# Rotary partners by buffer transfers instead of products with a constant matrix, in a two-block transformer kernel

## The chip, the cores and the metric

The kernel runs on one core of one Trainium2 chip. The metric is the device time of one execution in microseconds (us), as the median of three runs. The core has five engines that run side by side and wait for one another by semaphores: TensorE (PE, matrix products, with its weight loads as PEld), VectorE (DVE), ScalarE (ACT), GpSimd (POOL) and SyncE (SP). Transfers (DMAs) are issued by SP, ACT and POOL and carried out by 16 DMA engines that all queues share.

## The reference, cut to what matters

A sequence of 256 tokens with 1024 features goes through one block without rotary embedding and then through two layers (`l` = 0, 1), each of feed-forward, token mixer, feed-forward. The token mixer has three attention kinds of 8 heads: MOBA (here causal softmax attention), stick-breaking (SB) and latent attention (MLA). Rotary embedding is applied in two of them:

```python
def apply_rope(x, cos, sin):
    x1, x2 = jnp.split(x, 2, axis=-1)
    return jnp.concatenate([x1 * cos - x2 * sin, x1 * sin + x2 * cos], axis=-1)

def partial_rope(x, cos, sin):            # MOBA queries and keys: the first 16 of a head's 64 features
    return jnp.concatenate([apply_rope(x[..., :PARTIAL_ROT], cos, sin), x[..., PARTIAL_ROT:]], axis=-1)
# MLA: apply_rope on the 32 rotary features of each head's query, and on 32 features of a key that all heads share
```

Each rotated feature needs its partner: the feature 8 places away in MOBA (16 in MLA). The output is x * cos + partner * (plus or minus sin).

## The kernel before

Activations of a layer are kept with features on the 128 partitions and the 256 tokens along each partition. Moving a value to its partner feature therefore means moving it between partitions, which VectorE and ScalarE do not do in an elementwise operation. The kernel before does it with TensorE: it multiplies by a 128x128 matrix of 0, 1 and -1 (`rot_p` for MOBA, `rot_m` for MLA, both part of the constant block `dcon`), into the PSUM tile `nps`.

Weights come in chunks of 1 MB. SP loads chunk c into `raw` (three buffers). ACT rounds it to `hi` (`split`, L816), DVE subtracts to get `lo` (`split`, L1179), PE does three products per tile pair (hi x hi, hi x lo, lo x hi: L429 to L431), 48 matmuls of 256 columns for a chunk. The order on each engine is written out by hand; nothing is reordered by a scheduler.

In the token mixer, chunks and heads are interleaved in steps s (`mixing`). Ahead of step 0 stand the chunks `moba.q0`, `moba.k0`, `moba.v0`, `moba.q1` (each q or k chunk gives 256 features, that is 4 heads, as a 128x512 tile of `ra`; `v` is values). In step s PE does: the scores of head s (in pairs at even s), the value products of finished heads, the turning of the normalized weights of head s-1 (`turned`, L694, a transposition through `pt`), and then one weight chunk of the list: `moba.k1` in step 0, `moba.v1` in step 1, then the SB chunks, the latent chunks `lat.0` and `lat.1` (steps 8, 9), gates, `uq` in step 13 (MLA queries), `ukv` in step 14 (MLA keys and values). ACT and DVE treat the chunk of the step before: ACT copies it out of PSUM (`take`, L940 to L945), splits the chunk after next, does `exps` (L976) of head s and copies `pt` for head s-1 (L989). DVE does `largest` (L1336: adds the mask and takes the row minimum), its half of `split`, then whatever the dictionary `extra` names for this step, then `normed` (L1348, L1355: divides by the row sums), and some products for the modulation vectors (L1195, 1024 elements each).

The rotary steps stand in this frame as follows.

- PE: `rotary_moba` (L730) for q0 after `fm_first`, for k0 after the chunk v0, for q1 in step 0, for k1 in step 1. `rotary_mla` for the key in step 12 (L743) and for the query in step 14 (L748). All six share `nps`, so each waits for the rotation before it.
- DVE: `rotate_moba` (L1416 to L1419, three operations of 128x512: partner by sine, value by cosine, sum) for q0 and k0 before step 0, for q1 and k1 in steps 0 and 1 between `split` and `normed`. `rotate_mla_k` (L1423) in step 12, `rotate_mla_q` (L1430) in step 14, ahead of `take_v` (L1410), which empties the PSUM banks of `ukv` that PE needs for the next chunk but one.
- Who waits: the scores of head 0 wait for the rotation of k0, those of head 4 for k1. The turning of head 0 on PE waits for `normed` of head 0, which stands behind the rotation of q1 on DVE; the turning of head 1 waits for `normed` of head 1, behind the rotation of k1.

POOL issues the bias loads of the first block (L408) and, for each of eight vectors, a store to DRAM and a broadcast load back (L395, L402).

Of the kernel before, what the change touches and what calls it, by code (L numbers as in the profile page):

```python
# [10 lines left out]
ALU = mybir.AluOpType  # L11

P = 128
SEQ = 256
# [3 lines left out]
HD = 64  # L18
# [118 lines left out]
DCOL, NDCOL = columns(("neg_tri", P), ("neg_ones", P), ("rot_p", P), ("rot_m", P), ("cos_p", SEQ),  # L137
# [21 lines left out]
def program(nc, d, known):  # L159

    with ExitStack() as ctx:
# [85 lines left out]
        s_cond_b_in = signal("cond_b_in")  # L247
        s_out_stored = signal("out_stored")
# [4 lines left out]
        s_summed, s_rotated, s_across = signal("summed"), signal("rotated"), signal("across")  # L253
# [13 lines left out]
        s_glu = signal("glu")  # L267
# [10 lines left out]
        def flat2(ap):  # L278
            return ap.rearrange("p a t -> p (a t)")
# [23 lines left out]

        def values_of(l, kind):
            return m_v if kind == "mla" else qkv_of(l, kind)[2]

# [82 lines left out]
        def _(eng):  # L389
            nc.gpsimd.memset(eps[:], EPS).then_inc(*s_eps_made.up("eps"))  # L390
            def turned_row(tag, cols):
# [8 lines left out]
                if tag[2:] == "post1":  # L400
                    eng.wait_ge(*s_scored.at((tag[0], 3 * HEADS - 1)))
# [23 lines left out]
        def _(eng):  # L425
# [297 lines left out]
            def rotary_moba(l, n):  # L723

                c = AT[f"{l}.moba.{n}"]
                eng.wait_ge(*s_taken_a.at((c, 0)))
                if n != "q0":
                    eng.wait_ge(*s_rot.at((l, {"k0": "q0", "q1": "k0", "k1": "q1"}[n])))
                at = 4 * (n[0] == "k") + 2 * int(n[1])
                mm(nps[:], dcon[:, DCOL["rot_p"]], flat2(ra[:, at:at + 2, :]), start=True,  # L730
                   stop=True).then_inc(*s_rotated.up((l, n)))

# [6 lines left out]

            def rotary_mla(l, what):  # L740
                if what == "k":
                    eng.wait_ge(*s_r.at(l + ".lat"))
                    mm(nps[:, 0:SEQ], dcon[:, DCOL["rot_m"]], lat[:, 3, :], start=True,  # L743
                       stop=True).then_inc(*s_rotated.up((l, "mla k")))
                else:
                    eng.wait_ge(*s_taken_a.at((AT[f"{l}.uq"], 0)))
                    eng.wait_ge(*s_rot.at((l, "mla k")))
                    mm(nps[:], dcon[:, DCOL["rot_m"]], flat2(m_qr), start=True,  # L748
                       stop=True).then_inc(*s_rotated.up((l, "mla q")))
# [1080 lines left out]
```

## Time and profile before

| what | value |
|---|---|
| median of 3 runs | 1740.6 us (1739.4 to 1741.92) |
| profiled execution, its own time | 1739.8 us |
| its span | 1738.0 us |
| mean granted TensorE clock | 0.997 of full |
| PE busy | 1673.2 us, 96% |
| PEld busy | 1552.6 us, 89% |
| DVE busy | 1258.4 us, 72% |
| ACT busy | 875.1 us, 50% |
| POOL busy | 21.8 us, 1% |
| chain that ended last, by engine | PE 80%, DVE 6%, ACT 5%, DMA 3%, others 5% |

The span is the time from the first to the last instruction of the profiled execution; its own time is 1.8 us longer. The chain that ended last follows, from the last instruction back, what released each step. In the rows further down, each timeline row has the start in us from the span's start, the duration in us, engine, line, operation, and `output<-inputs`; `x2` is two instructions merged into the row, and the bracket at the end is idle time of that engine just before, with what ended it. Layer 0's mixer starts near 640 us, layer 1's near 1290 us, and the rows of the two are alike.

### The profile page before, as it was taken

The numbers are of one execution on the slowest core, as the hardware profiler recorded it, in microseconds if no ns is written. First come the engines' busy times: TensorE is split into PE (matmuls) and PEld (weight loads), VectorE is DVE, ScalarE is ACT, GpSimd is POOL, SyncE is SP. The second block draws the span as 40 slices with busy tenths as digits, with TensorE's granted clock in tenths as the row PEclk, the third lists the DMA queues.
The fourth block names the chain that finished last, engine by engine and source line by source line (L and its number), as shares of the span: only waits on it lengthen the run. The fifth ranks groups of instructions, "written<-read, shape, count | busy, mean of one in ns | idle before, by whom it ended". The sixth has DMA issues, their size and how long they took to land.

```text
span 1738.0 us, 29616 instructions
## 1 busy us (share of the span) xinstructions
PE 1673.2 (96%) x12356; PEld 1552.6 (89%) x12356; DVE 1258.4 (72%) x1813; ACT 875.1 (50%) x1241; POOL 21.8 (1%) x39
## 2 busy tenths in 40 slices
PE   2999999998999999999999999999999999999998
PEld 2999889987999889989989998999889989989996
DVE  6777879987787666666768875787666666768653
ACT  4555466654444365665473344534365665464432
POOL 0000000000000000000000000000000000000000
PEclk9999999999999999999999999999999999999999
DMA  9868646777677944755548786677744746537552
GB/s 384 309 254 247 241 168 236 208 294 280 217 290 280 289 171 170 209 191 200 214 146 290 283 240 241 229 282 288 291 162 169 220 180 214 205 147 272 186 179 108
DMA packets 70933, 398.92 MB, mean 230 GB/s; under 512 B 8208, under 2 KB 8464, under 8 KB 36112
## 3 DMA queue, kind: packets, MB, share of 16 engines
q1 hardware_dynamic: 67392, 386.06, 63.1%
q0 software_dynamic: 2976, 9.47, 1.6%
q8 instruction: 98, 1.61, 0.4%
q10 hardware_dynamic: 432, 1.50, 0.2%
q14 instruction: 35, 0.29, 0.0%
HBM read 395.92 MB, written 1.08 MB: 228 GB/s over the span
## 4 chain that ended last, share of the span: by engine, by line
PE 80%; DVE 6%; ACT 5%; DMA 3%; DVEq 2%; issue 2%; ACTq 1%; SPq 1%
PE lin L429 17%; PE lin L430 17%; PE lin L431 17%; PE att L564 17%; DVE lo L1179 3%; ACT hi L816 2%; PE att L667 2%; PE lin L467 2%; DMA raw<-in_w 2%; PE lin L469 2%; DMA ada_w<-in_ada 2%; PE lin L477 2%; DVEq L1508 1%; PE pt L694 1%; SPq L355 1%
## 5 line engine op out<-in xcount | busy, mean ns | idle before, releaser
L1179 DVE TENSOR_TENSOR lo<-raw,hi 128x2048 fp32r<-128x2048 f32 x262 | 600.1, 2291 | 288.6 <-ACT hi L816 288.4
L429 PE MATMUL lin<-h_hi,hi 128*128 128x256 f32 x2480 | 699.2, 282 | 2.4 <-DVE work L1503 1.6
L430 PE MATMUL lin<-h_lo,hi 128*128 128x256 f32 x2480 | 691.9, 279 | 0.0
L431 PE MATMUL lin<-h_hi,lo 128*128 128x256 f32 x2480 | 691.9, 279 | 0.0
L816 ACT ACTIVATE hi<-raw 128x2048 fp32r<-128x2048 f32 x262 | 500.5, 1911 | 209.7 <-PE att L564 133.6
L429 PEld LDWEIGHTS lin<-h_hi,hi 128*128 128x128 f32 x2480 | 466.3, 188 | 5.3 <-issue 5.1
L430 PEld LDWEIGHTS lin<-h_lo,hi 128*128 128x128 f32 x2480 | 466.3, 188 | 1.1 <-issue 1.0
L431 PEld LDWEIGHTS lin<-h_hi,lo 128*128 128x128 f32 x2480 | 466.1, 188 | 0.0
L1195 DVE CUSTOM_DVE_ANT_0 ada_w<-ada_w,cs 128x1024 f32<-128x1024 f32 x179 | 218.0, 1219 | 18.7 <-DMA ada_w<-in_ada 18.6
L1032 ACT ACTIVATE work<-lin 128x256 f32<-128x256 f32 x88 | 33.9, 385 | 280.1 <-PE lin L431 271.9
L564 PE MATMUL att<-hi,act_hi 128*128 128x512 f32 x440 | 135.6, 389 | 0.2 <-DVE lo L1179 0.2
L564 PE MATMUL att<-lo,act_hi 128*128 128x512 f32 x440 | 135.5, 389 | 0.0
L564 PE MATMUL att<-hi,act_lo 128*128 128x512 f32 x440 | 135.5, 389 | 0.0
L564 PEld LDWEIGHTS att<-lo,act_hi 128*128 128x128 f32 x440 | 82.6, 188 | 17.2
L564 PEld LDWEIGHTS att<-hi,act_lo 128*128 128x128 f32 x440 | 82.6, 188 | 17.2
L564 PEld LDWEIGHTS att<-hi,act_hi 128*128 128x128 f32 x440 | 82.1, 188 | 17.3 <-DVE lo L1179 0.6
L467 PE MATMUL lin<-h_hi,hi 128*128 128x256 f32 x240 | 59.4, 289 | 21.1 <-ACT h_hi L897 21.1
L467 PEld LDWEIGHTS lin<-h_hi,hi 128*128 128x128 f32 x240 | 46.9, 195 | 23.0 <-issue 23.0
L429 PE MATMUL lin<-br_hi,hi 128*128 128x256 f32 x224 | 64.1, 286 | 1.9 <-ACT ra L952 1.6
L430 PE MATMUL lin<-br_lo,hi 128*128 128x256 f32 x224 | 62.5, 279 | 0.0
L431 PE MATMUL lin<-br_hi,lo 128*128 128x256 f32 x224 | 62.5, 279 | 0.0
L469 PE MATMUL lin<-h_hi,lo 128*128 128x256 f32 x240 | 58.6, 285 | 0.0
(266 smaller groups left out, 2015.5 us busy)
## 6 DMA issues: line engine op xcount, KB each, us to landing
raw<-in_w SPq DMA_DIRECT2D x269, 1024.0 KB, 4.8
ada_w<-in_ada SPq DMA_DIRECT2D x179, 512.0 KB, 5.2
ada_s<-in_ada SPq DMA_DIRECT2D x13, 512.0 KB, 16.5
bias<-in_bias POOLq DMA_DIRECT2D x16, 256.0 KB, 4.7
ffn_row<-rows POOLq DMA_DIRECT2D x5, 512.0 KB, 9.7
x<-in_x ACTq DMA_DIRECT2D x1, 1024.0 KB, 6.8
dcon<-in_dcon SPq DMA_DIRECT2D x1, 1024.0 KB, 6.9
ra<-rows POOLq DMA_DIRECT2D x2, 512.0 KB, 5.0
```

Of the source, the lines that this page charges most:

```text
L429: mm(out, w_hi, a_hi, start=start, stop=False, skip_group_check=skip)
L430: mm(out, w_hi, a_lo, start=False, stop=False, skip_group_check=skip)
L431: return mm(out, w_lo, a_hi, start=False, stop=stop, skip_group_check=skip)
L467: mm(o, hi[c % SPLIT][:, b], h_hi[:, t, :], start=t == 0 and j == 0, stop=False, skip_group_check=True)
L469: mm(o, lo[c % SPLIT][:, b], h_hi[:, t, :], start=False, stop=False, skip_group_check=True)
L477: ins = mm(outs[i][:, j * SEQ:(j + 1) * SEQ], hi[c % SPLIT][:, b], h_lo[:, t, :], start=False, stop=t == 3, skip_group_check=True)
L564: ins = mm(att[:, 2 * a + n, :], act[:, t, tokens], w[s][:, kk * D + n * 512:kk * D + (n + 1) * 512], start=t == 0 and i == 0, stop=t == 2 ...
L667: ins = mm(out, q, k, start=start, stop=stop, skip_group_check=skip)
L816: act(hi[c % SPLIT][:], raw[:, c % RAW, :], ACT.Copy).then_inc(*s_hi.up(c))
L1032: act(work[2 + k % 2][:, 0:SEQ], lin[:, BANK[(c, 0)], 0:SEQ], ACT.Silu).then_inc(*s_gated.up((stage, k)))
L1179: tt(lo[c % SPLIT][:], raw[:, c % RAW, :], hi[c % SPLIT][:].bitcast(F32), ALU.subtract).then_inc(*s_lo.up(c))
L1195: ve.tensor_tensor_reduce(out=w, in0=w, in1=cs[:], scale=1.0, scalar=0.0, op0=ALU.mult, op1=ALU.add, accum_out=ada_out[:, h:h + 1]).then_i ...
```

## The change

The partner features are no longer a product. They are copied between partitions by small DMAs inside SBUF, and the sine table now carries the sign (negative for the first half of the rotated features).

- MOBA: for each of q0, k0, q1, k1, ACT issues four DMAs (`fetch_moba`), each of 8 partitions by 512 values (16 KB), from `ra` into `turn` (queries) or `lat_sq` (keys). They stand in ACT's order after the split that follows the chunk's `take`; for q1 and k1 they stand at the end of steps 0 and 1 (`late`), behind `exps`, and in step 1 also behind the copy of `pt`.
- MLA: POOL issues eight DMAs of 16 partitions for the key (256 values each) once `lat.1` is taken, and eight for the query (512 values each) once the first part of `uq` is taken, into free rows of `ra`. They stand between the store and the broadcast load of the row `post1`.
- DVE: `rotate` waits for the last of the DMAs instead of the product, and multiplies the partner tile in place, out of SBUF instead of PSUM. Since the MOBA transfers write only 16 of every 64 partitions, `clear_partners` sets `turn` and `lat_sq` to zero once per layer, after the last `swiglu` of the first feed-forward. `take_v` gets a `drain` in front.
- PE: `rotary_moba` and `rotary_mla` are gone, and with them the matrices in `dcon` (256 of its 2048 columns).

ACT, around steps 0 and 1 of the mixer. Before (`L940` and `L943` are the takes of q1 and k1, `L816` the split, `L976` the exps, `L989` the copy of `pt`):

```order
L940 ACTIVATE ra<-lin 128x512
L816 ACTIVATE hi<-raw 128x2048
L976 ACTIVATE work,den<-work,mn 128x128
L976 ACTIVATE work,den<-work,mn 128x256
L943 ACTIVATE ra<-lin 128x512
L816 ACTIVATE hi<-raw 128x2048
L976 ACTIVATE work,den<-work,mn 128x128
L976 ACTIVATE work,den<-work,mn 128x256
L989 ACTIVATE work<-pt 128x384
```

The same place after the change:

```order
L935 ACTIVATE ra<-lin 128x512
L811 ACTIVATE hi<-raw 128x2048
L988 ACTIVATE work,den<-work,mn 128x128
L988 ACTIVATE work,den<-work,mn 128x256
L947 DMA turn<-ra 8x512 x4
L938 ACTIVATE ra<-lin 128x512
L811 ACTIVATE hi<-raw 128x2048
L988 ACTIVATE work,den<-work,mn 128x128
L988 ACTIVATE work,den<-work,mn 128x256
L1001 ACTIVATE work<-pt 128x384
L947 DMA lat_sq<-ra 8x512 x4
```

Four transfers now follow the exps of head 0, and four follow the copy of `pt` in step 1.

PE, end of the chunk q1 and start of step 0. Before (`L667` are the scores of heads 0 and 1, `L730` the product with `rot_p` for q1, `L429` and `L430` the chunk k1):

```order
L431 MATMUL lin<-h_hi,lo 128x256
L667 MATMUL att<-ra 128x128 x2
L667 MATMUL att<-ra 128x256 x2
L730 MATMUL nps<-ra,dcon 128x512
L429 MATMUL lin<-h_hi,hi 128x256
L430 MATMUL lin<-h_lo,hi 128x256
```

After the change:

```order
L451 MATMUL lin<-h_hi,lo 128x256
L687 MATMUL att<-ra 128x128 x2
L687 MATMUL att<-ra 128x256 x2
L449 MATMUL lin<-h_hi,hi 128x256
L450 MATMUL lin<-h_lo,hi 128x256
L451 MATMUL lin<-h_hi,lo 128x256
```

Only the product is gone; the order of the rest stays.

The diff, cut to its core:

```diff
         @block.gpsimd
+            def fetch_mla(l, what):
+                eng.wait_ge(*s_taken_a.at((AT[f"{l}.lat.1" if what == "mla_k" else f"{l}.uq"], 0)))
+                src = lat[:, 3:4, :] if what == "mla_k" else m_qr
+                for to, fro, n, last in partner_rows(MLA_ROPE, MLA_ROPE):
+                    eng.dma_start(partner_of[what][to:to + n], src[fro:fro + n]).then_inc(
+                        *s_partner[what].up(*([(l, what)] if last else []), n=16))
...
                 if tag[2:] == "post1":
+                    fetch_mla(tag[0], "mla_k")
+                    fetch_mla(tag[0], "mla_q")
                     eng.wait_ge(*s_scored.at((tag[0], 3 * HEADS - 1)))
...
         @block.tensor
                 fm_first(l + ".pre1", f"{l}.moba.q0", f"{l}.moba.k0")
-                rotary_moba(l, "q0")
                 tm(f"{l}.moba.v0")
-                rotary_moba(l, "k0")
                 fm(f"{l}.moba.q1")
-                mixing(l, MIX_HEADS, MIX_SLOTS, {
-                    0: lambda: rotary_moba(l, "q1"), 1: lambda: rotary_moba(l, "k1"), 11: lambda: latent_sums(l),
-                    12: lambda: rotary_mla(l, "k"), 14: lambda: rotary_mla(l, "q")})
+                mixing(l, MIX_HEADS, MIX_SLOTS, {11: lambda: latent_sums(l)})
...
         @block.scalar
+            def fetch_partners(l, what, src):
+                dst, arrived = partner_of[what.split(".")[0]], s_partner[what.split(".")[0]]
+                for to, fro, n, last in partner_rows(16, HD):
+                    eng.dma_start(dst[to:to + n], src[fro:fro + n]).then_inc(
+                        *arrived.up(*([(l, what)] if last else []), n=16))
+
+            def fetch_moba(l, n):
+                c = AT[f"{l}.moba.{n}"]
+                at = 4 * (n[0] == "k") + 2 * int(n[1])
+                if n[1] == "0":
+                    eng.wait_ge(*s_cleared.at(l))
+                else:
+                    eng.wait_ge(*s_rot.at((l, n[0] + "0")))
+                eng.wait_ge(*s_taken_a.at((c, 0)))
+                fetch_partners(l, f"{n[0]}.{n[1]}", ra[:, at:at + 2, :])
...
                 for n in ("q0", "k0", "v0"):
                     take(f"{l}.moba.{n}")
                     split(AT[f"{l}.moba.{n}"] + SPLIT)
+                    if n != "v0":
+                        fetch_moba(l, n)
...
+                    0: [lambda: fetch_moba(l, "q1")], 1: [lambda: fetch_moba(l, "k1")],
                     9: [square_q], 10: [square_kv], 11: [latent_r], 12: [latent_first],
...
         @block.vector
+            def rotate(l, what, x_, cos, sin, done):
+                partner = partner_of[what.split(".")[0]]
+                n = x_.shape[1]
+                eng.wait_ge(*s_partner[what.split(".")[0]].at((l, what)))
+                tt(partner, partner, over(dcon[:, DCOL[sin]], n), ALU.mult)
+                tt(x_, x_, over(dcon[:, DCOL[cos]], n), ALU.mult)
+                ve.drain()
+                return tt(m_kr.unsqueeze(1) if what == "mla_k" else x_, x_, partner, ALU.add).then_inc(
+                    *s_rot.up((l, done)))
...
+            def clear_partners(l):
+                ve.memset(turn[:], 0.0)
+                ve.memset(lat_sq[:, 0:2, :], 0.0).then_inc(*s_cleared.up(l))
```

## Rows read from the trace of the kernel before

**Rows 1.** Head of the page.
```profile
span 1738.0 us, 29616 instructions
```

**Rows 2.** PE timeline, layer 0: products for q0 and k0, and a matmul behind.
```profile
640.62 1.02 PE L730 MATMUL nps<-ra,dcon 128*128 128x512 f32 x2
...
641.60 0.28 PE L430 MATMUL lin<-lo,h_hi 128*128 128x256 f32 x1
...
648.09 1.10 PE L730 MATMUL nps<-ra,dcon 128*128 128x512 f32 x2 [0.77 <-ACT ra L945]
```

**Rows 3.** PE timeline, steps 0 to 2: scores, turning of head 0, k1's product, turning of head 1.
```profile
654.72 0.93 PE L667 MATMUL att<-ra 64*128 64x128 f32 x8
...
662.28 0.55 PE L694 MATMUL pt<-con,work 128*128 128x128 f32 x3
663.04 1.12 PE L730 MATMUL nps<-ra,dcon 128*128 128x512 f32 x2 [0.22 <-ACT ra L943]
...
670.63 0.55 PE L694 MATMUL pt<-con,work 128*128 128x128 f32 x3
```

**Rows 4.** DVE timeline, k0's rotation and step 0.
```profile
653.35 0.69 DVE L1419 TENSOR_TENSOR ra<-ra,turn 128x512 f32<-128x512 f32 x1
655.67 0.29 DVE L1336 CUSTOM_DVE_ANT_0 work<-att,con 128x128 f32<-128x128 f32 x1 [1.63 <-PE att L667]
...
656.24 0.08 DVE L1336 DVE_READ_ACCUMULATOR2_ANT mn<- 128x1 f32 x1
657.25 2.29 DVE L1179 TENSOR_TENSOR lo<-raw,hi 128x2048 fp32r<-128x2048 f32 x1 [0.93 <-ACT hi L816]
659.46 0.68 DVE L1416 TENSOR_TENSOR turn<-nps,dcon 128x512 f32<-128x512 f32 x1
...
661.67 0.55 DVE L1355 TENSOR_SCALAR work<-work,rden 128x128 f32<-128x128 f32 x2
```

**Rows 5.** ACT timeline, first and last row of the exps of head 0.
```profile
657.12 0.39 ACT L976 ACTIVATE work<-work,mn 128x128 f32<-128x128 f32 x1
...
657.91 0.19 ACT L976 ACTIVATION_READ_ACCUMULATOR work<-work,mn 128x1 f32 x1
```

**Rows 6.** ACT's queue at the start: its first and third DMA issue.
```profile
0.73 0.41 ACTq L1040 DMA_DIRECT2D x<-in_x  x1
...
1.66 0.45 ACTq L1042 DMA_DIRECT2D con<-in_con  x1
```

**Rows 7.** From issue to landing of the stores `out_x` (256 and 512 KB).
```profile
DMA to landing us min/median/max: 2.6/2.6/2.7
```

**Rows 8.** From issue to landing of POOL's bias loads (256 KB, weight loads beside them).
```profile
DMA to landing us min/median/max: 2.7/4.7/8.6
```

**Rows 9.** DVE timeline, end of the latent step (12).
```profile
750.67 0.95 DVE L1446 TENSOR_TENSOR br_lo<-lat,br_hi 128x768 fp32r<-128x768 f32 x1
```

**Rows 10.** PE timeline, first matmul of the chunk `uq`.
```profile
751.84 0.36 PE L429 MATMUL lin<-br_hi,hi 128*128 128x256 f32 x1
```

**Rows 11.** PE's waits from 742 to 768 us: total, times, longest.
```profile
PE lin L429 <- ACT ra L958: 0.8, 1, 0.8
```

**Rows 12.** ACT timeline, the takes of the first two parts of `uq`.
```profile
755.04 1.08 ACT L952 ACTIVATE ra<-lin 128x512 f32<-128x512 f32 x2
```

**Rows 13.** DVE timeline, first operation of the MLA query's rotation.
```profile
763.36 0.68 DVE L1430 TENSOR_TENSOR turn<-nps,dcon 128x512 f32<-128x512 f32 x1
```

**Rows 14.** POOL's bias DMAs: durations min/median/max in ns.
```profile
L408 POOL DMA_DIRECT2D bias<-in_bias x16: 539/539/678, 29.7 to 144.5; - x16
```

**Rows 15.** POOL timeline, stores of the rows `post0` and `post1`.
```profile
568.29 0.92 POOL L395 DMA_DIRECT2D rows<-post_gain  x1 [218.28 <-DVE post_gain L1231]
...
719.73 0.91 POOL L395 DMA_DIRECT2D rows<-post_gain  x1 [140.00 <-DVE post_gain L1231]
```

**Rows 16.** DVE timeline, the operation beside the second store.
```profile
719.35 1.22 DVE L1195 CUSTOM_DVE_ANT_0 ada_w<-ada_w,cs 128x1024 f32<-128x1024 f32 x1
```

**Rows 17.** DVE timeline, the place where the partner tiles will be cleared.
```profile
569.32 2.29 DVE L1179 TENSOR_TENSOR lo<-raw,hi 128x2048 fp32r<-128x2048 f32 x1 [1.32 <-ACT hi L816]
```

More of the change, by code:

```diff
@@ L247, in program @@
         s_cond_b_in = signal("cond_b_in")
+        s_partner = {n: signal(f"partner_{n}") for n in ("q", "k", "mla_k", "mla_q")}
         s_out_stored = signal("out_stored")
@@ L266, in program @@
         s_z, s_scaled, s_h_hi_v = signal("z"), signal("scaled"), signal("h_hi_v")
[L267 removed]
+        s_glu, s_cleared = signal("glu"), signal("cleared")
         s_act, s_taps, s_merged, s_rot, s_lat = (signal("act_made"), signal("taps"), signal("merged"), signal("rot"),
@@ L302, in program, with partner_rows @@
         m_v = ra[:, 11:15, :].rearrange("p a t -> p (a t)").rearrange("p (u n) -> p u n", u=2)
+        partner_of = {"q": turn[:], "k": lat_sq[:, 0:2, :], "mla_k": ra[:, 14:15, :], "mla_q": ra[:, 12:14, :]}
         def values_of(l, kind):
             return m_v if kind == "mla" else qkv_of(l, kind)[2]
+        def partner_rows(n_rot, width):
+            half = n_rot // 2
+            moves = [(base + to, base + half - to, half) for base in range(0, P, width) for to in (0, half)]
+            return [m + (i == len(moves) - 1,) for i, m in enumerate(moves)]
         def by_token(ap):
@@ L721, in values @@
                 ins.then_inc(*s_pv.up((l, s + 1)))
[L723 to L731, printed above, removed]
             def latent_sums(l):
@@ L738, in latent_sums @@
                 mm(nps[:, SEQ:2 * SEQ], ones, sq[:, 2, :], start=True, stop=True).then_inc(*s_summed.up(l + ".lat"))
[L740 to L749, printed above, removed]
             def mixing(l, heads, slots, extra):
@@ L1587, in _ @@
                 layer_post(l, 0)
+                clear_partners(l)
                 for k in range(FD - 1):
@@ L1662, in constants, with rotary @@
     c[:, DCOL["neg_ones"]] = -1.0
-    def rotary(n_rot, width, rot, cos, sin):
+    def rotary(n_rot, width, cos, sin):
         inv = (f(500000.0) ** (-np.arange(0, n_rot, 2, dtype=f) / n_rot)).astype(f)
@@ L1671, in rotary @@
             for r in range(n_rot):
-                row, partner = base + r, base + (r + half) % n_rot
-                m[partner, row] = -1.0 if r < half else 1.0
-                cc[row], ss[row] = np.cos(ang[:, r % half]), np.sin(ang[:, r % half])
-        c[:, DCOL[rot]], c[:, DCOL[cos]], c[:, DCOL[sin]] = m, cc, ss
-    rotary(16, HD, "rot_p", "cos_p", "sin_p")
-    rotary(MLA_ROPE, MLA_ROPE, "rot_m", "cos_m", "sin_m")
+                row = base + r
+                cc[row], ss[row] = np.cos(ang[:, r % half]), np.sin(ang[:, r % half]) * (-1 if r < half else 1)
+        c[:, DCOL[cos]], c[:, DCOL[sin]] = cc, ss
+    rotary(16, HD, "cos_p", "sin_p")
+    rotary(MLA_ROPE, MLA_ROPE, "cos_m", "sin_m")
     short = lambda m: np.concatenate([m.T[0:P, :], m.T[P:, P:]], 1)
```

25 lines of the change are left out of this document (6 added, 19 removed).

## The prediction

> **What bounds the kernel now.** I read the shares first: TensorE is busy for 96% of the span and carries 80% of the chain that ended last, so a microsecond taken from PE is worth a microsecond, unless what PE then waits for is not ready. Then the timelines of PE, DVE and ACT around the places that the change touches, in layer 0, and last the landing times of the transfers. The reader should see that PE has almost no idle time around steps 0 and 1, but that the engines behind it are only just in time: DVE's `normed` of head 0 ends at 662.22 us (661.67 + 0.55) and PE starts to turn that head at 662.28 [rows 3, 4]. All sums are made in layer 0 and taken twice. The profiled execution took 1739.8 us (span 1738.0 us [rows 1] and 1.8 us around it), the median of the runs is 1740.6 us; I add my difference to the median.
>
> **What goes from PE.** The product for q0 starts at 640.62 us, and the second matmul behind it at 641.60 us; with 0.12 us for the first one, it holds PE for 0.86 us, in two records of the trace [rows 2]. k0 costs the same and 0.77 us of waiting for ACT's take in front [rows 2]; q1 the same; k1 the same and 0.22 us of waiting [rows 3]. That is 4 x 0.86 + 0.99 = 4.4 us for each layer, 8.9 us in all. MLA follows below. Whether any of it reaches the end depends on who is late next, so I rebuild steps 0 and 1.
>
> **Before step 0.** PE reaches the chunk v0 0.86 us earlier, and ACT's take of v0, DVE's split and the rotation of k0 all follow it. The rotation ended at 654.04 us (653.35 + 0.69) [rows 4]; it will end at 653.2 us. PE will be through the chunk q1 at 654.7 - 0.86 - 0.86 - 0.77 = 652.2 us and wait 1 us. The scores of heads 0 and 1 start at 653.25 us instead of 654.72 us [rows 3]: 1.5 us won of 2.5 us. The transfers for q0 and k0 are asked for 4 us and more after they are issued, behind DVE's splits, so I cost them at nothing. ACT's issues lie beside its split if its queue goes on while the split runs; if not, ACT falls 1.8 us behind for each four, and 0.8 us of the gain goes.
>
> **Step 0.** From the scores to the turning of head 0, PE needed 662.28 - 654.72 = 7.56 us [rows 3], without the product 6.6 us (here it took nearer 0.97 us), so PE is ready at 659.85 us. DVE: `largest` ended at 656.32 us; 1.47 us earlier is 654.85 us. Before, the exps started at 657.12 us because ACT was still in its split (its `hi` came for DVE at 657.25 us [rows 4]); that split follows the chunk q1 and now ends at 654.7 us, so the exps start at 654.95 us. DVE's split runs from 654.95 to 657.2 us. The four transfers for q1 stand behind the exps, which take 1.0 us (657.12 to 658.10 [rows 5]). First issue: between 655.0 us, if ACT's queue runs ahead, and 655.95 us; I take 655.5. Issues follow each other by (1.66 - 0.73) / 2 = 0.465 us [rows 6], so the fourth is issued 1.4 us later, at 656.9 us.
>
> How long until it lands? No row shows a copy inside SBUF. Stores of 256 KB on quiet engines land after 2.6 us [rows 7]; at the rate of about 400 GB/s they would need 0.65 us for the data, which leaves an estimate of 1.95 us for a small one. Loads of 256 KB on a second queue beside weight loads land after 2.7 to 8.6 us, 4.7 in the middle [rows 8]. I take 2.3 us, between the estimate and the quiet row, since a 16 KB piece is nearer to these; the bounds are 1.95 and 4.7 us. The Trainium skill, page "DMA: Bandwidth & Descriptors", section "Anatomy of one DMA — SWDGE (gpsimd) path", gives a fixed part of about 2.0 us for each DMA; that is for the GpSimd path, no run here shows it for SBUF to SBUF, and the sum with it would be 0.3 us for each of the two waits, 1.2 us in all, below mine.
>
> So the partner lands at 659.2 us, and DVE, free since 657.2, waits 2 us. From the start of the rotation to the end of `normed` it needs 662.22 - 659.46 = 2.76 us [rows 4]: 661.95 us instead of 662.22. PE, ready at 659.85, waits 2.1 us, and is then ahead by only 0.3 us. Nearly all that was won up to here is given back.
>
> **Step 1.** Call the end of `normed` T. DVE does `largest` to T + 0.6 and its split to T + 2.9. ACT does the exps of head 1 and the copy of `pt` from T + 0.65 to T + 2.0, with the transfers for k1 behind them: first issue between T + 0.7 and T + 2.0, I take T + 1.3. The fourth lands at T + 1.3 + 1.4 + 2.3 = T + 5.0, `normed` of head 1 ends at T + 7.75. PE took 670.63 - 662.28 = 8.35 us from one turning to the next [rows 3], without the product and its wait 7.25 us. It waits 0.5 us and gains 0.6 us. With 0.3 us from step 0 this is 0.9 us ahead; I round to 1.0 us a layer, with bounds from the placing of the first issue and the landing: -2.3 us (both early, 1.95 us) to +4 us (4.7 us). From step 2 on PE is bound as before, so this difference stays.
>
> **MLA.** The key's product (half as long, 0.43 us) stands before a chunk that is followed by `uq`. But `uq` starts at 751.84 us, and what it needs, DVE's `br_lo`, ends at 751.62 us [rows 9, 10]: 0.1 us is won. The eight transfers were issued 20 us before. The query's product (0.86 us) stands before `ukv`, where PE waits 0.8 us for ACT to empty a bank [rows 11]; ACT's order does not get earlier, so the wait grows by what the product frees: nothing won. POOL's eight query transfers start when ACT's take ends at about 755.65 us [rows 12]. At 0.54 us each [rows 14] the last is issued at 759.45 us and lands at 761.8 us; DVE asks at 763.36 us [rows 13]. If it comes later, `take_v` behind it is late, and PE with it. The drain in `take_v` costs under 0.1 us. MLA together: 0, between -0.2 and +3 us a layer.
>
> **Clearing.** Two memsets of 128x512, at the length of the 128x512 operations of DVE at most 0.69 us each [rows 4], fall at a place where DVE waits 1.32 us for ACT [rows 17]. Without that cover they would delay one split by 1.4 us, in a stage in which each split is followed by another wait for ACT. Nothing. The shorter `dcon` load is far ahead of its use: nothing.
>
> **Sum.** -1.0 us a layer, -2.0 us in all: 1737.8 us by the profiled execution, 1738.6 us by the median. 8.9 us of PE work leave and about 7 us of it turn into waits for the partner's way through ACT's queue, DMA and DVE.
>
> **Rivals.**
> A. The partners are there when DVE asks. Then `normed` of head 0 ends at 657.2 + 2.76 = 659.95 us, 2.3 us earlier, and in step 1 DVE's own chain (T + 7.3 against 7.25) gives another 1.1 us: 3.4 us a layer, 6.8 in all, 1733.8 us. For it: DMA engines are lightly used here. Against it: four issues in a row behind the exps leave the landing less than 1 us.
> B (slower). The small pieces queue behind the 1 MB weight loads. Place: DVE's waits for q1 and k1. Landing at 4.7 us [rows 8] instead of 2.3 adds 2.4 us at each of four waits: +9.6 - 2.0 = +7.6, 1748.2 us. The change turns into a loss above 2.8 us of landing time, and a measurable one above 3.7 us. Against it: by my times the weight load of each step is issued after the pieces.
> C (slower). POOL's query transfers are late. If its issues wait while DVE runs operations with two inputs (a split of 2.3 us and one of 1.2 us fall there), the last lands near 766.3 us, 3 us late: +6 - 2 = +4, 1744.6 us. Against it: POOL's store beside exactly such an operation took 0.91 us, and one with DVE idle 0.92 us [rows 15, 16]. The Trainium skill, page "SBUF — State Buffer", section "SBUF: two separate sides", says that GpSimd and VectorE share a port pair as an exclusive lock, and that VectorE in some operations keeps GpSimd from writing descriptors; the rows speak against it for this operation, so by them it gets a small chance.
> D. ACT stalls at its issues and other small losses eat the rest: within 1 us of before, 1740.6 us.
>
> **Chances.** Forecast 0.48, A 0.18, B 0.15, C 0.10, D 0.09. A measurement of this kernel can tell 0.2%, 3.5 us, from no change. The forecast's own range is 1736 to 1741 us: mostly the same, with 0.10 faster. A counts as faster; of B 0.11 and of C 0.07 as slower; D as the same. Faster 0.28, same 0.54, slower 0.18. The range 1733.5 to 1745 us takes in A, C and the weak half of B.
>
> **What would show it.** In the profile after: DVE's first operation of the q1 rotation waits for a DMA by 1 to 3 us, in both layers, and PE waits about 2 us for `normed` before it turns head 0, and near 0.5 us before head 1. PE waits about 1 us for k0's rotation ahead of the scores. No wait stands before the MLA rotations, the key's and the query's. The PE rows of L730, L743 and L748 are gone, while the stretch from the chunk v0 to the turning of head 1 is shorter by about 1 us only. It would be wrong if DVE finds the partner there (A), if its waits are over 3.5 us (B), if the MLA query's rotation waits (C), or if another place than these moves by over 1 us.

## The result and the profile after

The changed kernel takes 1756.8 us (median of 4 runs, 1754.2 to 1762.0) beside 1741.3 us (4 runs, 1739.4 to 1743.4) of the kernel before on the same chip: the ratio is 1.0098, with a 95% interval from 1.0080 to 1.0117. It is 15.6 us slower, where 2 us faster was forecast and 1745 us was the upper end of the range.

The page after starts with the span (before: [rows 1]) and shows one thing that is new: the clock granted to TensorE has a dip to 8 in two of the 40 slices, one in each layer's mixer.

```profile
span 1760.2 us, 29638 instructions
...
PEclk9999999999999998999999999999998999999999
```

This profiled execution, 1762.0 us, was the slowest of the four, and some 6 us of its difference lie outside the mixers, so I compare stretches and not ends. POOL's stores of the modulation rows stand in both traces: one ahead of the mixer and one in step 8, past the four MOBA rotations ([rows 15]: 568.29 and 719.73 us); the row load at the end of the MLA heads closes a second stretch (a row is read as start, length, engine, line, operation, and in brackets the idle time before it with what ended it). That load before, on POOL's timeline:

```profile
820.60 0.54 POOL L402 DMA_DIRECT2D ra<-rows  x1 [99.95 <-PE att L667]
```

The POOL timeline after:

```profile
571.06 0.91 POOL L413 DMA_DIRECT2D rows<-post_gain  x1 [219.62 <-DVE post_gain L1246]
...
730.38 0.91 POOL L413 DMA_DIRECT2D rows<-post_gain  x1 [148.55 <-DVE post_gain L1246]
...
766.49 3.81 POOL L406 DMA_DIRECT2D ra<-ra  x8 [21.91 <-ACT ra L964]
831.46 0.58 POOL L422 DMA_DIRECT2D ra<-rows  x1 [61.16 <-PE att L687]
```

The same two stretches in every kernel of this study, both layers, in us (of one profiled execution each; the ratio is of all runs):

| kernel | store to store, layer 0 / 1 | store to row load, layer 0 / 1 | timed, ratio to before (95%) |
|---|---|---|---|
| before | 151.4 / 151.4 | 100.9 / 100.5 | 1 |
| changed | 159.3 / 158.3 | 101.1 / 101.9 | 1.0098 (1.0080 to 1.0117) |
| e1_load_waits | 151.8 / 149.7 | 101.2 / 101.2 | 1.0020 (1.0011 to 1.0029) |
| e2_no_moba_copies | 148.3 / 148.3 | 101.1 / 100.7 | 0.9975 (0.9964 to 0.9986) |
| e3_pe_kept_busy | 158.4 / 156.3 | 102.4 / 104.0 | 1.0100 (1.0083 to 1.0117) |
| e4_rotate_later | 148.2 / 147.6 | 101.7 / 101.1 | 0.9965 (0.9952 to 0.9978) |
| e5_fetch_early | 153.6 / 148.2 | 101.2 / 100.9 | 0.9997 (0.9984 to 1.0009) |
| e6_last_piece_only | 148.9 / 148.0 | 101.2 / 101.4 | 0.9980 (0.9971 to 0.9990) |
| e7_mla_only | 151.4 / 151.3 | 103.8 / 100.8 | 1.0022 (1.0014 to 1.0031) |
| e8_pool_and_later | 146.4 / 146.3 | 100.3 / 100.3 | 0.9936 (0.9923 to 0.9950) |
| e9_products_later | 150.9 / 150.9 | 100.8 / 100.6 | 0.9987 (0.9978 to 0.9996) |
| e10_pool_only | 149.5 / 148.7 | 101.4 / 101.3 | 0.9980 (0.9971 to 0.9988) |
| e11_later_from_scalar | 147.2 / 146.0 | 100.3 / 100.3 | 0.9939 (0.9925 to 0.9952) |

So the loss is 7.9 and 6.9 us in the stretch with the MOBA rotations, 0.2 and 1.4 us in MLA's: 16.4 us together, the timed 15.6. Inside that stretch in layer 0, the DVE timeline answers to [rows 4]:

```profile
655.89 0.69 DVE L1436 TENSOR_TENSOR ra<-ra,lat_sq 128x512 f32<-128x512 f32 x1
657.60 0.29 DVE L1351 CUSTOM_DVE_ANT_0 work<-att,con 128x128 f32<-128x128 f32 x1 [1.01 <-PE att L687]
...
658.16 2.29 DVE L1194 TENSOR_TENSOR lo<-raw,hi 128x2048 fp32r<-128x2048 f32 x1
665.65 0.69 DVE L1433 TENSOR_TENSOR turn<-turn,dcon 128x512 f32<-128x512 f32 x1 [5.21 <-DMA turn<-ra]
...
667.86 0.55 DVE L1370 TENSOR_SCALAR work<-work,rden 128x128 f32<-128x128 f32 x2
...
676.91 0.69 DVE L1433 TENSOR_TENSOR lat_sq<-lat_sq,dcon 128x512 f32<-128x512 f32 x1 [5.74 <-DMA lat_sq<-ra]
```

DVE waits 5.2 and 5.7 us for the last piece of q1 and of k1 (5.2 and 5.4 in layer 1). PE, where [rows 3] have no wait before L694, pays for it (L714 is that line now):

```profile
656.64 0.93 PE L687 MATMUL att<-ra 64*128 64x128 f32 x8 [1.78 <-DVE ra L1436]
668.47 0.90 PE L714 MATMUL pt<-con,work 128*128 128x128 f32 x3 [5.11 <-DVE work L1370]
676.91 0.93 PE L687 MATMUL att<-ra 64*128 64x128 f32 x8
679.73 0.55 PE L714 MATMUL pt<-con,work 128*128 128x128 f32 x3 [1.90 <-DVE work L1370]
```

When were the pieces issued? ACT's timeline (ACTq: its issues), with SP's issue of the next weight chunk beneath:

```profile
642.44 3.23 ACTq L947 DMA_DIRECT2D turn<-ra  x4
645.71 0.60 ACT L938 ACTIVATE ra<-lin 128x512 f32<-128x512 f32 x1 [1.56 <-issue]
...
658.34 0.63 ACTq L947 DMA_DIRECT2D turn<-ra  x1
...
659.00 0.63 ACTq L947 DMA_DIRECT2D turn<-ra  x1
...
659.66 1.29 ACTq L947 DMA_DIRECT2D turn<-ra  x2
```

```profile
660.47 11.05 SPq L360 DMA_DIRECT2D raw<-in_w  x2
```

The fourth piece is issued at about 660.32 us (659.66 plus the spacing of 0.66), 0.15 us ahead of the 1 MB weight load. In step 1 even the issue of the load comes first, by 0.25 us: the fourth piece goes at 670.13 + 2 x 0.66 = 671.45 us.

```profile
670.13 1.97 ACTq L947 DMA_DIRECT2D lat_sq<-ra  x3
671.20 0.33 SPq L360 DMA_DIRECT2D raw<-in_w  x1
```

Back in step 0, the DMA view of 656 to 668 us, in slices of 0.3 us, shows what became of that lead:

```profile
DMA  0289999990002020209048999999600000000000
GB/s 0 109 355 437 410 437 437 437 437 0 0 0 55 0 48 7 48 7 218 0 191 328 382 410 437 437 437 410 280 21 0 0 0 0 0 0 0 0 0 0
```

The first three pieces' bytes move at 659.6, 660.2 and 660.8 us, about 1.3 us after each issue. By that the fourth is due near 661.6 us, but the load's first bytes come at 661.4 us (218 GB/s), 0.9 us after its issue, and then the full stream to 664.6 us. By queue (q1 is SP's, q10 ACT's; packets, MB, share of the engines' time), first from 661.3 to 664.5 us, where q10 has no packet, then from 664.5 to 665.6 us:

```profile
q1 hardware_dynamic: 123, 1.01, 87.7%
```

```profile
q1 hardware_dynamic: 21, 0.04, 9.6%
q10 hardware_dynamic: 16, 0.02, 4.2%
```

All 16 packets of a 16 KB piece move behind the stream, from 664.57 us on. DVE is released at 665.65 us. A lead at the issue was no lead at the engines. Where the piece stands in the meantime the trace does not show; it shows only when packets move.

### The profile page after: what moved, and what is told of

Same layout as the page of the kernel before. It is cut to its first block, busy times and chain, and to the rows that moved or that the text cites. A ratio compares the mean times of both kernels' runs of the same rounds, so it can differ in the third digit from the quotient of the medians.

```text
span 1760.2 us, 29638 instructions
## 1 busy us (share of the span) xinstructions
PE 1675.0 (95%) x12332; PEld 1558.3 (89%) x12332; DVE 1260.1 (72%) x1817; ACT 875.7 (50%) x1241; POOL 37.2 (2%) x71
## 4 chain that ended last, share of the span: by engine, by line
PE 75%; DVE 7%; ACT 5%; DMA 5%; DVEq 3%; issue 2%; ACTq 2%; SPq 1%; POOL 0%
PE att L584 17%; PE lin L449 16%; PE lin L450 16%; PE lin L451 16%; DVE lo L1194 3%; ACT hi L811 2%; PE att L687 2%; PE lin L487 2%; DMA raw<-in_w 2%; PE lin L489 2%; DVEq L1527 1%; PE pt L714 1%; PE lin L497 1%; DMA ada_w<-in_ada 1%; SPq L365 1%
```

## The experiments

**1. Do the small pieces queue behind the weight load?** In e1 SP holds the weight load of steps 0 and 1 back until the pieces have landed:

```diff
+                for l in "01":
+                    if c == AT[f"{l}.moba.q1"] + 6:
+                        eng.wait_ge(*s_partner["q"].at((l, "q.1")))
+                    if c == AT[f"{l}.moba.k1"] + 6:
+                        eng.wait_ge(*s_partner["k"].at((l, "k.1")))
                 eng.dma_start(raw[:, c % RAW, :], d["w"][c]) ...
```

> The changed kernel with one wait more on SP: the 1 MB weight load that was issued beside the partner pieces of q1 (and the next, beside those of k1) is issued only when the last piece has landed. Theory Q (the last pieces queue behind that load on the shared DMA engines): the last piece lands about 2.3 us after its issue instead of 5.3, DVE's waits for q1 and k1 fall from 5.2 and 5.7 us to 2 to 3 us, PE's waits for normed from 5.1 and 1.9 us to about 2 and 1 us, the clock stays up, and about 7 us a layer come back: 1741 to 1744 us, not slower than before by more than 3 us. Rival L (a copy inside SBUF has a fixed latency near 5 us on ACT's queue): waits unchanged, 1757 us or more.

Measured 1744.6 us (1741.7 to 1746.4). DVE's waits fell to 1.9 and 1.3 us (layer 1: 1.9 and 1.6), the DVE timeline:

```profile
663.32 0.69 DVE L1438 TENSOR_TENSOR turn<-turn,dcon 128x512 f32<-128x512 f32 x1 [1.87 <-DMA turn<-ra]
...
671.97 0.69 DVE L1438 TENSOR_TENSOR lat_sq<-lat_sq,dcon 128x512 f32<-128x512 f32 x1 [1.25 <-DMA lat_sq<-ra]
```

The last piece of q1 was issued at 661.33 us and released DVE at 663.3: 2.0 us, where it took 5.3 us in the changed kernel (660.32 to 665.65). A fixed latency of 5 us is out. The last piece of k1 took 3.2 us (668.77 to 671.97) with no weight load beside it; experiment 10 shows what stood there. 0.78 of the 0.98% are won back by this alone.

**2. What does the change win if nothing is waited for?** e2 leaves out MOBA's transfers and the waits for them (MOBA has no partner term then); DVE's operations and MLA stay.

```diff
                     split(AT[f"{l}.moba.{n}"] + SPLIT)
-                    if n != "v0":
-                        fetch_moba(l, n)
...
-                    0: [lambda: fetch_moba(l, "q1")], 1: [lambda: fetch_moba(l, "k1")],
...
-                eng.wait_ge(*s_partner[what.split(".")[0]].at((l, what)))
+                if what[:3] == "mla":
+                    eng.wait_ge(*s_partner[what].at((l, what)))
```

> The changed kernel without the 32 MOBA transfers and without DVE's waits for them; the rotation multiplies what stands in the cleared tile, so the MOBA part has no partner term. The MLA transfers stay. If the loss is the transfers' way and what follows from it (both Q and L): DVE starts each rotation as soon as its split is done, PE waits under 1 us in steps 0 and 1, 1734 to 1737 us (my rival A, 6.8 us under before, plus 1 us for MLA). If part of the loss sits elsewhere (the in-place multiplications out of SBUF, the memsets, the drain), it stays above 1741 us.

Measured 1736.4 us (1735.8 to 1738.3). Store to store is 3.1 us shorter than before, of the 4.4 us of products and their waits that went (ACT's issues are gone here as well). PE still waits for k0's rotation (1.2 us) and for DVE's `normed` (0.6 us), which is what is late next.

**3. Does the granted clock carry part of the loss?** After PE's wait of 5.1 us the clock fell; the stretches of the changed kernel (columns: stretch, its length, busy us of each engine, clock, DMA share, GB/s):

```profile
663.50:668.50 5.00, 0.03 (x1) 0.03 (x1) 2.70 (x7) 2.29 (x2) 0.00 (x0) 0.82 0.23 95
668.50:672.00 3.50, 3.50 (x17) 3.50 (x18) 2.67 (x5) 1.36 (x5) 0.00 (x0) 0.50 0.05 9
672.00:676.00 4.00, 4.00 (x30) 4.00 (x30) 0.00 (x0) 0.00 (x0) 0.00 (x0) 0.81 0.82 270
676.00:680.00 4.00, 2.10 (x19) 1.57 (x18) 2.94 (x9) 2.40 (x2) 0.00 (x0) 1.00 0.01 4
680.00:684.00 4.00, 4.00 (x23) 4.00 (x22) 3.61 (x10) 1.36 (x5) 0.00 (x0) 0.57 0.15 25
```

0.50 is 1.2 GHz: PE does 17 matmuls in 3.5 us there, and 71 in the 8 us from 684 us. In e3 PE multiplies 11 and 7 times into an unused tile ahead of the turning of heads 0 and 1:

```diff
+                    if l != "o" and s in (1, 2):
+                        for _ in range((11, 7)[s - 1]):
+                            mm(nps[:, 0:SEQ], ones, con[:, 0:SEQ], start=True, stop=True)
                     if 0 <= s - 1 < n:
```

> The changed kernel with 11 and 7 products of 128x256 into the unused bank nps ahead of the turning of heads 0 and 1 in each layer, to fill PE's waits. Theory C (after its 5 us wait PE runs at half clock for some us, which costs 3.5 us a layer): DVE's waits stay at 5 to 6 us, the granted clock stays at 1.00 through steps 0 to 2, 1749 to 1752 us. Rival (the slow stretch lies beside waits anyway and costs nothing): 1757 us or more.

Measured 1759.1 us (1758.2 to 1759.5), no gain. The clock from 664 us on was full, as these stretches of e3 show:

```profile
664.00:668.00 4.00, 4.00 (x20) 3.53 (x19) 2.81 (x9) 2.17 (x2) 0.00 (x0) 1.00 0.01 3
668.00:672.00 4.00, 4.00 (x35) 3.90 (x34) 2.56 (x4) 1.37 (x5) 0.00 (x0) 1.00 0.18 25
```

It gave store to store back 1.0 and 2.0 us, far less than I expected. In layer 0 this kernel has a slow stretch of its own in an earlier place (mean clock 0.86 from 652 to 657 us and 0.85 from 657 to 664 us), in layer 1 it has none there. The MLA stretch of that kernel was 1.3 and 2.1 us longer. DVE waits 1.8 and 2.0 us there for the MLA query's pieces, where the changed kernel waits 0.6 and 1.4, and in layer 1 PE runs at 0.50 from 1434 to 1437 us, behind a wait of 2.2 us.

Why did the clock cost so little? In step 1 the way goes `normed` of head 0, exps, issues, the queue, DVE, and PE is not on it. A slow PE from 668 to 676 us lies beside DVE's own wait of 5.7 us; only the stretch after 680 us (0.57 of 4 us) is on the path. That reading is argued, and its size, 0.43 x 4 = 1.7 us, agrees with the 1.0 and 2.0 us.

**4. Ask later.** e4 lets DVE turn q1 and k1 two steps later (they are needed by head 4):

```diff
-                    0: [lambda: rotate_moba(l, "q1")], 1: [lambda: rotate_moba(l, "k1")], 8: ...
+                    2: [lambda: rotate_moba(l, "q1")], 3: [lambda: rotate_moba(l, "k1")], 8: ...
```

> The changed kernel with DVE's rotations of q1 and k1 moved from steps 0 and 1 to steps 2 and 3, before the scores of head 4 need them. Transfers as they are. Theory Q and L alike: the pieces have landed by then, DVE does not wait, PE does not wait for normed, the clock stays up; what is left is ACT's delay before step 0 and MLA: 1735 to 1738 us, faster than before by 3 to 6 us. Rival: DVE has no room in steps 2 and 3 (2 us each) and the wait reappears there, 1741 us or more.

Measured 1735.9 us (1733.3 to 1736.6), faster than before by 0.35%. q1's last piece queues as in the changed kernel: it is issued at 656.93 us, the weight load at 657.08 us, and its packets move from 661.2 us on. Nobody waits for it. In step 1 the pieces are now 2 us ahead of the load.

**5. Issue earlier.** e5 moves ACT's issues ahead of the exponentials:

```diff
                     split(AT[f"{l}.{name}"] + SPLIT)
+                    if l != "o" and s < 2:
+                        fetch_moba(l, ("q1", "k1")[s])
...
-                    0: [lambda: fetch_moba(l, "q1")], 1: [lambda: fetch_moba(l, "k1")],
```

> As the changed kernel, but ScalarE issues the four pieces of q1 and of k1 right behind its taking and splitting of the same product, ahead of the head's exponentials, so some 2 us earlier; nothing else is moved. Queueing (the last piece's bytes stand behind the step's 1 MB weight load): all four are issued before the load is, the last lands about 2 us after its issue, VectorE waits for them under 1 us in steps 0 and 1 (5.2 and 5.7 us in the changed kernel), the exponentials run some 2.6 us later, and the kernel takes 1736 to 1741 us. A fixed latency of 5 us for such a piece: VectorE still waits about 3 us a step and the time is near 1750 us.

Measured 1741.0 us (1736.8 to 1744.9), at the edge of the expected range. q1's wait is gone, k1's is 1.5 us in layer 0; the waits from 650 to 690 us:

```profile
PE pt L714 <- DVE work L1371: 2.2, 1, 2.2
...
PE att L687 <- DVE ra L1437: 1.8, 1, 1.8
DVE lat_sq L1434 <- DMA lat_sq<-ra: 1.5, 1, 1.5
```

The pieces of q1 (issued from 657.37 to 659.35 us) show the queueing behind a load that was issued before them, at 656.43 us. The first was due at 658.65 us, 1.28 us after its issue, but from 658.6 to 660.4 us only the load's queue has packets, and all 64 packets of the four pieces follow between 660.5 and 661.2 us:

```profile
q1 hardware_dynamic: 93, 0.76, 100.0%
```

This costs nothing, since DVE asks at 662.4 us. In layer 1 the stretch store to store is as short as e2's (148.2 us), in layer 0 it is 5.3 us longer. There DVE waits the 1.5 us for k1, and TensorE runs slow twice, which it does not in layer 1; how much each costs is not shown. The stretches of layer 0:

```profile
657.00:664.00 7.00, 5.58 (x35) 4.99 (x36) 5.59 (x11) 3.07 (x6) 0.00 (x0) 0.76 0.57 171
676.00:680.00 4.00, 4.00 (x23) 4.00 (x22) 3.63 (x10) 1.36 (x5) 0.00 (x0) 0.57 0.28 39
```

**6. One piece instead of four.** e6 sends only the last piece of q1 and k1 (the partners of the other three groups of rows are left out), so it is issued 2.0 us sooner than the last of four:

```diff
-                for to, fro, n, last in partner_rows(16, HD):
+                for to, fro, n, last in partner_rows(16, HD)[(3 if what[-1] == "1" else 0):]:
```

> Of the four pieces of q1 and of k1 only the last is sent (the partner features of three of the four row groups are left out), with the same waits and the same place in ScalarE's order. Queueing: that one piece is issued 1.9 us earlier than the last of four was, so ahead of the weight load; it lands about 2 us after its issue, VectorE waits under 0.5 us for it, and the kernel takes 1736 to 1740 us. A latency that belongs to one such transfer whatever stands beside it: VectorE waits over 3 us a step and the kernel takes 1748 us or more.

Measured 1739.2 us (1736.5 to 1741.5). The DVE timeline has no wait at all before either rotation:

```profile
659.01 0.69 DVE L1433 TENSOR_TENSOR turn<-turn,dcon 128x512 f32<-128x512 f32 x1
...
666.70 0.69 DVE L1433 TENSOR_TENSOR lat_sq<-lat_sq,dcon 128x512 f32<-128x512 f32 x1
```

The same transfer of 16 KB, asked for in the same place, is in time when it comes to the DMA engines ahead of the load (its packets move at 658.3 us, the load is issued at 659.1 us).

**7. MLA alone.** e7 is the kernel before with MLA's two products replaced and MOBA's kept (the two `rotary_mla` calls go, `fetch_mla` and the changed `rotate_mla_k` and `rotate_mla_q` come in):

```diff
-                    0: ..., 1: ..., 11: lambda: latent_sums(l),
-                    12: lambda: rotary_mla(l, "k"), 14: lambda: rotary_mla(l, "q")})
+                    0: ..., 1: ..., 11: lambda: latent_sums(l)})
```

> The kernel before with MLA's two rotations by transfers from POOL and MOBA's still by the product with the constant matrix. By the changed kernel's trace the MLA stretch (from the third piece's row load to the fourth's) costs 0.2 us in layer 0 and 1.4 us in layer 1: 1742.3 us, between 1741 and 1743.5. If the MLA half were what costs (my prediction gave it up to 3 us a layer): 1745 us or more. If it wins its two products and nothing waits: 1739.5 us.

Measured 1745.5 us (1742.9 to 1747.9): a loss of 0.2%, and 2 us above the range that I expected (1741 to 1743.5). In layer 0 the last of the query's pieces was issued at 761.19 us and released DVE at 766.83; the waits there:

```profile
PE lin L446 <- DVE ra L1427: 2.0, 1, 2.0
...
PE lin L446 <- ACT ra L974: 1.6, 1, 1.6
DVE ra L1447 <- DMA ra<-ra: 1.5, 1, 1.5
```

DVE waits for the pieces, `take_v` stands behind, PE needs its banks, and its stretch is 2.9 us longer. Part of that is the clock, which is at 1.2 GHz behind PE's wait of 2.0 us (in the kernel before it is 1.00 there):

```profile
771.00:774.00 3.00, 3.00 (x16) 3.00 (x16) 2.93 (x4) 0.56 (x2) 0.00 (x0) 0.50 0.10 19
```

In layer 1 DVE waits 0.3 us and the stretch is 0.3 us longer. How late the pieces are depends on what the loads do at that moment: in layer 0 three loads follow each other from 758.5 to 768.4 us.

**8. A version in which the askers stand further back.** e8 has POOL issue MOBA's pieces, DVE turn q1 and k1 in steps 2 and 3, k0 ahead of its split for v0, and the MLA query's partner in `lat_sq`, turned in step 15 behind `take_v`:

```diff
-        partner_of = {..., "mla_q": ra[:, 12:14, :]}
+        partner_of = {..., "mla_q": lat_sq[:, 0:2, :]}
...
+                if tag[2:] == "post0":                    # POOL
+                    for n in ("q0", "k0", "q1", "k1"):
+                        fetch_moba(tag[0], n)
...
+                    if i == 2:                            # DVE, ahead of v0's split
+                        rotate_moba(l, "k0")
...
-                    0: [... "q1"], 1: [... "k1"], 8: ..., 14: [lambda: rotate_mla_q(l)]})
+                    2: [... "q1"], 3: [... "k1"], 8: ..., 15: [lambda: rotate_mla_q(l)]})
```

> All four of MOBA's transfers of a layer are issued by POOL, none by ScalarE; VectorE turns q1 and k1 in steps 2 and 3 and k0 ahead of v0's split; the MLA query's partner lies in lat_sq and is turned one step later, in step 15, after V is taken. With no transfer that VectorE asks for before it has landed, and ScalarE's queue free of issues: a mixer as with MOBA's transfers left out or better, 1731 to 1736 us, so 0.3 to 0.5% under the kernel before and no slower than the version that only turns later (1735.9). If ScalarE's issues cost nothing there and the MLA query's later place holds up the MLA heads: 1737 to 1740 us.

Measured 1730.8 us (1728.7 to 1732.8), 0.64% under the kernel before, the best of the study. Store to store is 5.1 us shorter than before in both layers, the MLA stretch 0.6 and 0.3 us. One wait for a landing stays, 1.6 us of DVE for k0's piece ahead of step 0, and it reaches nobody: PE has no wait from 640 to 690 us.

**9. Is that gain the later places' own?** e9 is the kernel before with the same move of q1 and k1, on PE (products in steps 2 and 3) and on DVE.

```diff
-                    0: lambda: rotary_moba(l, "q1"), 1: lambda: rotary_moba(l, "k1"), 11: ...
+                    2: lambda: rotary_moba(l, "q1"), 3: lambda: rotary_moba(l, "k1"), 11: ...
```

> The kernel before, with its products, but q1 and k1 multiplied and turned in steps 2 and 3 instead of 0 and 1, on TensorE and on VectorE. It tells how much of what the transfers won with the later places is the places' own. The transfers with the later places took 1735.9 us, 0.35% under the kernel before. If the gain comes from the products leaving TensorE: four products a layer stay, so 1739 to 1742 us, no change. If it is the place alone (VectorE is free in steps 0 and 1 for head 0 and 1): 1735 to 1737 us.

Measured 1738.8 us (1736.8 to 1742.4), ratio 0.9987. So about a third of e4's 0.35% is the place's own (0.13%, with an interval from 0.04 to 0.22%); the rest, and e8's further gain, comes with the transfers. e8 changes four things at once, and what each adds to e4 is not shown.

**10. Only the issuing engine, and with it the time of issue.** e10 is the changed kernel with e8's POOL part alone.

```diff
+                if tag[2:] == "post0":                    # POOL
+                    for n in ("q0", "k0", "q1", "k1"):
+                        fetch_moba(tag[0], n)
...
-                    0: [lambda: fetch_moba(l, "q1")], 1: [lambda: fetch_moba(l, "k1")],   # ACT
```

> The changed kernel with one difference: MOBA's pieces are issued by POOL, as soon as ScalarE has taken the product, not by ScalarE behind the head's exponentials; VectorE turns them in steps 0 and 1 as in the changed kernel. Queueing: the pieces are issued 2 to 3 us before the step's 1 MB weight load and land before VectorE asks, with no wait or one under 1 us; ScalarE's queue is free of them; 1734 to 1738 us. If the small pieces are slow by themselves, or POOL's issues are held up by VectorE: waits of over 2 us in steps 0 and 1 and 1744 us or more.

Measured 1737.3 us (1734.8 to 1740.6). POOL has nothing to wait for but ACT's take and the rotation whose tile it fills, and issues each piece in 0.5 us. Its rows, and DVE's, in which q1 has no wait:

```profile
651.26 1.98 POOL L413 DMA_DIRECT2D turn<-ra  x4 [8.89 <-DVE ra L1436]
659.17 1.97 POOL L413 DMA_DIRECT2D lat_sq<-ra  x4 [5.93 <-ACT ra L958]
```

```profile
655.00 0.69 DVE L1433 TENSOR_TENSOR turn<-turn,dcon 128x512 f32<-128x512 f32 x1
...
663.83 0.69 DVE L1433 TENSOR_TENSOR lat_sq<-lat_sq,dcon 128x512 f32<-128x512 f32 x1 [1.08 <-DMA lat_sq<-ra]
```

k1's last piece still needs 3.2 us (660.65 to 663.83), with no weight load beside it. By queue from 661.7 to 662.9 us, then from 662.1 to 662.9 us (q0 is POOL's):

```profile
q0 software_dynamic: 32, 0.02, 8.0%
q8 instruction: 1, 0.02, 4.6%
```

```profile
q0 software_dynamic: 2, 0.00, 2.0%
```

A single packet of 16 KB on the queue that the profile calls `instruction` moves from 661.76 to 662.63 us, on one engine, and the piece's last 2 of 32 packets come right behind it. k1's last piece in e1 and e5 has the same: its last 2 packets of 16 follow such a packet. That the one holds up the other is read from the times; no run removes it.

The step from 1.0098 to 0.9980, over 1% of the time, is won by POOL issuing the same pieces, 2 to 3 us earlier. e5, which moves ACT's issues earlier by about 2 us and nothing else, wins most of it (0.9997).

**11. Later, but from ACT.** e11 is e8 with MOBA's pieces issued by ACT in the changed kernel's places.

```diff
-                if tag[2:] == "post0":                    # POOL, as e8 has it
-                    for n in ("q0", "k0", "q1", "k1"):
-                        fetch_moba(tag[0], n)
...
+                    0: [lambda: fetch_moba(l, "q1")], 1: [lambda: fetch_moba(l, "k1")],   # ACT
```

> As the fastest version so far (1730.8 us) but MOBA's pieces issued by ScalarE, in the places of the changed kernel; the later turnings and the MLA query's partner in lat_sq stay. It tells what POOL's issues are worth once no landing is waited for. ScalarE's 16 issues a layer at 0.63 us fill its queue, and its next product is taken some 1.5 us later: 1733 to 1736 us, between the two. If the issuing engine doesn't matter: 1730 to 1732 us.

Measured 1731.0 us (1730.2 to 1732.7), the same as e8. Once nobody waits for a landing, ACT's 16 issues a layer cost nothing that can be measured.

## Why the prediction was wrong

**The step that failed** is the landing of the fourth piece in steps 0 and 1. I gave it 2.3 us with 4.7 us as a bound, and put rival B aside with "by my times the weight load of each step is issued after the pieces". In step 0 the order of the issues was right: 0.3 us of lead by my times, 0.15 us in the trace. In step 1 it was not: 0.2 us of lead by my times, and the load was issued 0.25 us ahead of the fourth piece. And the lead counts at the DMA engines and not at the issue: there the load was first in both. The landing took 5.3 us instead of 2.3, above the bound. Rival B named the place and the mechanism, with a price from rows 8 that was too small (2.4 us a wait; q1's piece shows 5.3 us in the changed kernel against 2.0 in e1). The prediction's own sign of it, DVE's waits over 3.5 us, came true. The other half of the argument, "DMA engines are lightly used here", weighed a mean (0.33 from 655 to 662 us before) where one full stream was enough. [Rows 8] were themselves a warning: the same bias load landed after 2.7 us or after 8.6 us, according to the weight loads beside it, and I used their middle as if it were one latency. What the prediction had right is the undisturbed piece: 1.95 us by its estimate, 2.0 us for q1 in e1.

**Point by point, layer 0**, in times less 2.8 us (by which this execution was already late at the first store):
- Before step 0: scores at 653.9 us, forecast 653.25; ACT did stall at its issues (1.56 us of idle before it takes k0), the 0.8 us that I had named. PE waited 1.78 us, forecast 1.
- First piece issued at 655.6, forecast 655.5. Spacing 0.66 us, forecast 0.465 from [rows 6]: the fourth at 657.5 instead of 656.9.
- Landing 662.9 instead of 659.2; from there to the end of `normed` the 2.76 us of [rows 4] held. PE turned head 0 at 665.7 instead of 661.95: 3.75 us late.
- Step 1: 11.26 us from turning to turning (668.47 to 679.73), forecast 7.75: 3.5 us late, with the fourth piece issued 3.0 us after T (forecast 2.7) and landed 5.5 us later (forecast 2.3).
- Clock: 1.7 us after 680 us, in no term of mine (an estimate from the granted clock; e3 bears it out with 1.0 and 2.0 us).
- Sum: -1.0 + 3.75 + 3.5 + 1.7 = +7.95 us, measured 7.9. That it closes to 0.1 us is luck, since the clock's term is known only to 1 us.
- What the change is worth with nothing waited for was sized well: 3.4 us a layer in rival A, 3.1 us in e2.

**MLA** was given 0, from -0.2 to +3 us a layer. Measured 0.2 and 1.4 in the changed kernel, 2.9 and 0.3 in e7. PE's wait for ACT's take grew from 0.8 ([rows 11]) to 1.6 us, by the product's 0.86, as said. The query's pieces landed at 774.3 us, about 4.5 us after the last issue, and not after 2.3, and DVE waited 0.6 and 1.4 us where I had put no wait: the same error as above. POOL's issues took 0.48 to 0.51 us each (3.81 us for eight); one that fell beside DVE's split of 2.29 us in e10 took 0.50, as those with DVE idle. So rival C's lock did not show, and a loss of its size came, in e7, with pieces that landed 5.6 us after the last issue among loads. **Clearing** cost nothing: two memsets of 0.48 us, and DVE's wait for ACT behind them fell from 1.32 ([rows 17]) to 0.28 us.

The Trainium skill, page "DMA: Bandwidth & Descriptors", section "Queues, rings and completion order", says that each DMA engine takes turns between the queues it has work for, and drains a whole packet, typically 9 to 17 descriptors, before it switches. Whether the trace agrees hangs on what a packet is. If it were one packet as the profile counts them, a row of 8 KB in 0.31 us, the pieces would have slipped into the load, and they did not: from 661.3 to 664.5 us q1 had 123 rows and q10 none, in e5 93 and none. But the load is 128 rows of 8 KB on 16 engines, 8 for each engine and one small one that ends it, and if such a row is what the Trainium skill calls a descriptor, an engine's share of the load is one packet of 9. Then the Trainium skill and the trace agree: a piece waits for the engine's share of the load ahead, and comes in between two loads. POOL's MLA key pieces fit this too: from 745 to 750 us, among loads without a pause, they had 252 rows beside q1's 350. That the two words mean the same thing no run here shows. The Trainium skill, same page, section "Issuing engines are not separate DMA queues", says that all issuers' transfers run on the same 16 engines and that a second issuer saves only the time of issuing. That holds here: moving the issues from ACT to POOL changed the time by nothing (e8 and e11) when their time of issue did not matter.

## What to carry to other kernels

A small transfer that is waited for has no latency of its own: find the large load nearest to it in time, and count from the moment at which both reach the DMA engines, not from the issue. When products leave TensorE for transfers, either the consumer moves behind or the issue moves forward. The same copies cost 0.98% when they were asked for at once and landed 5 us later; they won 0.35% when only the consumer moved two steps back (e4), 0.20% when POOL issued them earlier (e10), and 0.64% with both and the MLA query moved as well (e8). A lead of a few tenths of a microsecond in a hand-made schedule is to be priced as if it were lost.

## What the runs showed of the hardware

- A 16 KB copy inside SBUF (8 partitions of 2 KB) lands 2.0 us after its issue with nothing beside it (q1 in e1), and 5.1 to 5.5 us after it when a 1 MB load is issued within 0.3 us of it (four cases, q1 and k1 of both layers).
- Its first bytes move 1.28 us after the issue on ACT's queue. If a weight load is under way then, they move behind it: k0's four pieces of the changed kernel, issued from 646.40 to 648.38 us, have no packet until 650.4 us, the load has all of the engines' traffic from 647.6 to 650.4 us. q1's pieces in e5 show the same.
- A single 16 KB packet of the queue `instruction` takes 0.9 us on one engine, and a piece that lands 3.2 us after its issue (k1 in e1 and e10) has its last 2 packets behind it.
- The issue of such a copy takes 0.63 us on ACT's queue, against 0.41 to 0.45 us for the 128-partition loads of [rows 6], and 0.48 to 0.51 us on POOL's.
- ACT went on with its split while the four issues ran, but stood 1.56 us before the operation behind them.
- After a PE wait of 5.1 us the granted clock was 0.50 (1.2 GHz), and after one of 1.9 us it was 0.57 in the mean of the stretch from 680 to 684 us. After one of 2.0 us in e7 it was 0.50 from 771 to 774 us. After the wait of 1.8 us before the scores it stayed at 1.00 in the changed kernel and was 0.72 in the mean from 658 to 664 us in e1. The last two waits are of the same length, so the length alone does not decide.
